# Hybrid attention stepped by head pair, with its output projection split by inner halves

## The reference, cut to what matters

```python
h = x
n = rms_norm(h, attn_norm[0])
proj = n @ w_in                                  # 1024 x 3080
oa = dilated_attention(rope(qa)*s, rope(ka), va) # 8 heads of 64
ob = forgetting_attention(qb*s, kb, vb, logf)    # 8 heads of 64
h = h + concat([oa, ob]) @ w_out                 # 1024 x 1024
h = h + conv_glu_ffn(rms_norm(h, ffn_norm[0]), ...)
...
```

## Time and profile before

| | |
|---|---|
| median of 3 runs | 2890.99 us |
| the profiled execution | 2890.38 us |
| its span, first to last instruction | 2888.4 us |
| TensorE busy | 2715.4 us, 94% |
| VectorE / ScalarE / GpSimd busy | 60% / 36% / 35% |
| mean granted TensorE clock | 0.961 of full |
| hybrid attention | 93.2 to 285 us |
| `out0` gemms | 285 to 328.6 us |
| first feed-forward gemms of layer 0 | from 334 us |

### The profile page before, as it was taken

How to read it: one execution, slowest core, us unless ns; L and a number is a source line. 1 busy time by engine, 2 the same in 40 slices (tenths; PEclk the granted TensorE clock), 3 DMA queues, 4 the chain that set the end, 5 groups by cost and what they waited for, 6 DMA issues and landing times.

```text
span 2888.4 us, 34721 instructions
## 1 busy us (share of the span) xinstructions
PE 2715.4 (94%) x11434; PEld 2001.0 (69%) x11434; DVE 1733.4 (60%) x2250; ACT 1052.6 (36%) x1644; POOL 1018.7 (35%) x383
## 2 busy tenths in 40 slices
PE   8999999999998999999698998999989898899998
PEld 6654788887764678888475465888757644687875
DVE  3645774576486676377558346828635944583672
ACT  3344332233144232232442445323344244432333
POOL 3210344444321244444143123444424411354452
PEclk9997999999998899999899999999999998999999
DMA  4110223232210123232111011222321110122221
GB/s 151 59 45 22 73 95 102 94 106 84 73 55 33 46 93 101 89 101 95 47 52 52 29 44 61 99 89 93 104 66 59 44 44 22 66 94 96 93 98 69
DMA packets 56406, 212.17 MB, mean 73 GB/s; under 512 B 6400, under 2 KB 6656, under 8 KB 56192
## 3 DMA queue, kind: packets, MB, share of 16 engines
q1 hardware_dynamic: 55456, 209.60, 21.8%
q10 hardware_dynamic: 864, 1.44, 0.2%
HBM read 208.92 MB, written 2.10 MB: 73 GB/s over the span
## 4 chain that ended last, share of the span: by engine, by line
PE 74%; DVE 11%; ACT 5%; issue 5%; POOL 4%; DVEq 0%; ACTq 0%; DMA 0%; POOLq 0%; SPq 0%
PE bank_G L501 20%; PE bank_G L503 20%; PE bank_G L502 19%; PE bank_S L1141 5%; POOL wlo L449 3%; PE bank_O L1151 2%; DVE conv_up L764 2%; PE bank_X L1161 2%; PE bank_S L548 1%; ACT whi L474 1%; PE bank_X L1706 1%; DVE mx L2037 1%; DVE prod L784 1%; PE bank_X L833 1%; DVE conv_up L763 1%
## 5 line engine op out<-in xcount | busy, mean ns | idle before, releaser
L449 POOL TENSOR_TENSOR wlo<-raw,whi 128x1024 fp32r<-128x1024 f32 (+1 forms) x361 | 975.9, 2704 | 1739.7 <-ACT whi L474 1739.6
L501 PE MATMUL bank_G<-n_hi,whi 128*128 128x512 f32 x2392 | 975.9, 408 | 63.9 <-DVE n_lo L608 24.7
L503 PE MATMUL bank_G<-n_hi,wlo 128*128 128x512 f32 x2392 | 944.0, 395 | 0.0
L502 PE MATMUL bank_G<-n_lo,whi 128*128 128x512 f32 x2392 | 942.7, 394 | 0.0
L501 PEld LDWEIGHTS bank_G<-n_hi,whi 128*128 128x128 f32 x2392 | 457.3, 191 | 204.3 <-issue 60.0
L474 ACT ACTIVATE whi<-raw 128x1024 fp32r<-128x1024 f32 (+1 forms) x363 | 403.4, 1111 | 349.7 <-PE bank_G L503 349.6
L502 PEld LDWEIGHTS bank_G<-n_lo,whi 128*128 128x128 f32 x2392 | 457.7, 191 | 96.6 <-issue 7.8
L503 PEld LDWEIGHTS bank_G<-n_hi,wlo 128*128 128x128 f32 x2392 | 455.7, 191 | 98.8
L674 DVE SCALAR_TENSOR_TENSOR h<-h,mixed 128x512 f32 (+1 forms) x96 | 70.3, 732 | 397.1 <-ACT mixed L480 397.1
L501 PE MATMUL bank_G<-a_hi,whi 128*128 128x512 f32 x704 | 275.3, 391 | 5.7 <-DVE a_lo L786 3.8
L503 PE MATMUL bank_G<-a_hi,wlo 128*128 128x512 f32 x704 | 274.0, 389 | 0.0
(11 more groups left out here) (271 smaller groups left out, 2659.4 us busy)
## 6 DMA issues: line engine op xcount, KB each, us to landing
raw<-in_w_mix_in SPq DMA_DIRECT2D x42, 512.0 KB, 3.3
raw<-in_w_out SPq DMA_DIRECT2D x32, 512.0 KB, 3.3
raw<-in_w_hyb_in SPq DMA_DIRECT2D x25, 512.0 KB, 3.3
raw<-in_w_diff_in SPq DMA_DIRECT2D x24, 512.0 KB, 3.3
raw<-in_w_up0a SPq DMA_DIRECT2D x22, 512.0 KB, 3.3
raw<-in_w_up0b SPq DMA_DIRECT2D x22, 512.0 KB, 3.3
raw<-in_w_up1a SPq DMA_DIRECT2D x22, 512.0 KB, 3.2
raw<-in_w_up1b SPq DMA_DIRECT2D x22, 512.0 KB, 3.3
```

The lines of the kernel that those rows point to most:

```text
L449: pool.tensor_tensor(b.wlo[:, g.slot, 0:width], b.raw[:, g.slot, 0:width], b.whi[:, g.slot, 0:width], ALU.subtract).then_inc(b.lo_ready, 1)
L501: pe.matmul(out, b.whi[:, g.slot, w], hi[:, k, :], start=(k == 0), stop=False)
L502: pe.matmul(out, b.whi[:, g.slot, w], lo[:, k, :], start=False, stop=False)
L503: mm = pe.matmul(out, b.wlo[:, g.slot, w], hi[:, k, :], start=False, stop=(k == pieces - 1))
```

## The change

1. `out0` becomes two groups of eight half-width tiles: `out0a` (inner channels 0 to 511, the dilated heads) and `out0b` (the forgetting heads). Both add to `h`.
2. The hybrid attention runs 32 units of a head pair (two heads by one query block) in 37 steps, lag 2 in place of 3. The two score matmuls of a step read partitions 0 to 63 and 64 to 127 and write the two slots of `bank_S`. A gemm half (12 matmuls) stands in each of steps 0 to 23; steps 24 to 26 have none; step 27+m has the gemm of `out0a` tile m; steps 35 and 36 have three quarters of `out0b` tiles 0 and 1. `hyb_out_pe` does the rest.
3. No projection's result is copied to `mixed` any more (except in the mixers' inputs): VectorE adds `bank_G` to `h` directly and that evacuates the slot. ScalarE only splits weights there.
4. In `out0b`, ScalarE does the squares, and the next gemm's inputs 0 to 3 are made between the tiles, 4 to 7 after the last.
5. `norm_sum` 1, 2 and 3 move behind the first gemm of the next group.

```diff
-GROUPS = [("hyb_in", B1_IN, W8), ("out0", KD, W8), *ffn_groups(0),
+KH = KD // 2
+GROUPS = [("hyb_in", B1_IN, W8), ("out0a", KD, KH * P), ("out0b", KD, KH * P), *ffn_groups(0),
...
-def first_gemms_n(pe, b, g0, nlo):
+def first_gemms_n(pe, b, g0, nlo, q=None):
     gemm(pe, b, Index(g0), b.n_hi, b.n_lo, KD, lambda k: pe.wait_ge(b.nlo_ready, nlo + k + 1))
+    if q is not None:
+        norm_sum(pe, b, q)
     gemm_n(pe, b, Index(g0 + 1))
...
@@ products_act
-            wait(act, b.resid_done, r0 + k - 1 if k else max(r0 - 1, 0))
-            take(act, b, Index(g0 + k), b.mixed[:, (g0 + k) % 2, :])
+            split_hi(act, b, Index(g0 + k + 2))
...
@@ products_dve
-        dve.wait_ge(b.evacuated, g.at(1))
-        ins = dve.scalar_tensor_tensor(h, h, float(alpha), b.mixed[:, g.slot, :], ALU.mult, ALU.add).then_inc(b.resid_done, 1)
+        dve.wait_ge(b.gemm_done, g.at(1))
+        dve.scalar_tensor_tensor(h, h, float(alpha), b.G[:, g.slot, :], ALU.mult, ALU.add).then_inc(b.evacuated, 1)
...
-LAG = (3, 2, 3, 3)
+LAG = (2, 2, 3, 3)
+EARLY = 6
+PARKED_STEPS = {24: (0, 1), 25: (2, 3), 27: (4,), 29: (5,)}
+OUT_STEP = 27
...
+def hyb_scores_pe(pe, b, a, u):
+    o, i = a.unit(u)
+    if u % NB == 0:
+        qk_ready_pe(pe, b, a, o)
+    wait(pe, b.masked, 2 * u)
+    for x in range(2):
+        q, k = b.qk[a.rows(x), a.tile(o), i * P:(i + 1) * P], b.qk[a.rows(x), a.tile(o) + 4, 0:a.keys(i)]
+        mm = pe.matmul(b.S[:, x, 0:a.keys(i)], q, k, start=True, stop=True)
+    mm.then_inc(b.scored, 1)
...
+    for step in range(a.steps):
+        u, w, t = step, step - a.lag - 1, step - a.lag
+        if u < a.units:
+            hyb_scores_pe(pe, b, a, u)
+        if 0 <= w < a.units and w % NB == NB - 1:
+            hyb_values_pe(pe, b, a, w // NB)
+        if 0 <= t < a.units:
+            hyb_transposes_pe(pe, b, a, t)
...
+        m = step - OUT_STEP
+        if 0 <= m < KD:
+            gemm(pe, b, Index(outa + m), b.n_hi, b.n_lo, KH, (lambda k: pe.wait_ge(b.nlo_ready, 8 + k + 1)) if m == 0 else None)
+        elif KD <= m < KD + 2:
+            hyb_out_part_pe(pe, b, m - KD, range(KH - 1))
...
+def hyb_out_act(act, b):
+    g0, tiles = group_tiles("out0b")
+    for m in range(tiles):
+        split_hi(act, b, Index(g0 + m + 2))
+        act.wait_ge(b.evacuated, g0 + m + 1)
+        if m < KH:
+            gained_hi_act(act, b, "ffn_norm0", m)
+        wait(act, b.resid_summed, m - 1)
+        act.activation(b.sq[:, (m + 1) % 2, :], b.h[:, m, :], ACT.Square).then_inc(b.resid_squared, 1)
+    for m in range(KH, KD):
+        gained_hi_act(act, b, "ffn_norm0", m)
...
+        if 0 <= step - OUT_STEP < KD:
+            residual_dve(dve, b, Index(outa + step - OUT_STEP), step - OUT_STEP)
...
-            norm_sum(pe, b, 1)
-            ffn_pe(pe, b, 0, 16)
-            norm_sum(pe, b, 2)
+            hyb_out_pe(pe, b)
+            ffn_pe(pe, b, 0, 16, 1)
```

More of the change, by code:

```diff
@@ L1045, in plan @@
         self.lead = 2
[L1046 to L1056, removed]
+        self.rotated = 16
+        self.qk0 = FIRST["diff_in"] + 8
+        plan_qk(self)
         order = [("rot", n) for n in range(2 * self.lead - 1)]
@@ new lines, in hyb_values_pe @@
+def hyb_values_pe(pe, b, a, o):
+    for x in range(2):
+        taken_out(pe, b, Index(a.posts[NB * o + NB - 1][x]))
+    wait(pe, b.hyb_taken, min(max(o - 1, 0), EARLY))
+    for j in range(NB):
+        for x in range(2):
+            h = 2 * o + x
+            mm = pe.matmul(b.O[a.rows(x), o % 2, j * P:T], b.v[:, j, h * DH:(h + 1) * DH], b.pt[:, x, j, j * P:T],
+                           start=(j == 0), stop=(j == NB - 1), skip_group_check=True)
+            if j == NB - 1:
+                mm.then_inc(b.headed, 1)
@@ new lines, in hyb_transposes_pe, with hyb_fox_pe @@
+def hyb_transposes_pe(pe, b, a, t):
+    o, i = a.unit(t)
+    for x in range(2):
+        p = Index(a.posts[t][x])
+        pe.wait_ge(b.scaled, 2 * t + x + 1)
+        wait(pe, b.x_free[p.slot], p.turn())
+        for j in range(i + 1):
+            mm = pe.transpose(b.X[:, p.slot, j * P:(j + 1) * P], b.probs[:, a.small(t, x), j * P:(j + 1) * P], b.k["ident"])
+        mm.then_inc(b.posted, 1)
+def hyb_fox_pe(pe, b, a, o):
+    pe.wait_ge(b.fox, 5)
+    for x in range(2):
+        p, n = Index(a.fox_posts[o][x]), 2 * o + x - 8
+        pe.wait_ge(b.x_free[p.slot], p.turn())
+        pe.matmul(b.X[:, p.slot, :], b.k["ident"][0:8, n:n + 1].to_broadcast([8, P]), b.negc[0:8, :],
+                  start=True, stop=True).then_inc(b.posted, 1)
@@ L1282, in hyb_attention_pe @@
 def hyb_attention_pe(pe, b):
-    qk_ready_pe(pe, b, ATT_HYB, 0)
+    a, outa, outb = ATT_HYB, FIRST["out0a"], FIRST["out0b"]
     taken_out(pe, b, Index(POST_HYB + 7))
[L1286 to L1295, removed]
@@ new lines, in hyb_out_part_pe, with hyb_out_pe @@
+def hyb_out_part_pe(pe, b, m, part):
+    gemm(pe, b, Index(FIRST["out0b"] + m), b.n_hi, b.n_lo, KH,
+         (lambda k: pe.wait_ge(b.nlo_ready, 8 + KH + k + 1)) if m == 0 else None, part, KH)
+def hyb_out_pe(pe, b):
+    g0, tiles = group_tiles("out0b")
+    for m in range(2):
+        hyb_out_part_pe(pe, b, m, range(KH - 1, KH))
+    for i, g, g_next in pairs(pe, g0 + 2, tiles - 2):
+        gemm(pe, b, g, b.n_hi, b.n_lo, KH, None, None, KH)
+        gemm(pe, b, g_next, b.n_hi, b.n_lo, KH, None, None, KH)
@@ new lines, in hyb_out_act @@
+def hyb_out_act(act, b):
+    g0, tiles = group_tiles("out0b")
+    for m in range(tiles):
[7 more added lines that the diff above has]
+        gained_hi_act(act, b, "ffn_norm0", m)
+def hyb_attention_dve(dve, b, link):
+    a, outa = ATT_HYB, FIRST["out0a"]
+    for step in range(a.steps):
+        u, t, w = step, step - a.lag + 1, step - a.lag - 3
+        scaling = 0 <= t < a.units
+        if scaling:
+            dve.wait_ge(b.exped, t + 1)
+            n = a.small(t, 0)
+            r = b.rden[:, n:n + 2]
+            link.mark(dve.reciprocal(r, b.den[:, n:n + 2]))
+        for x in range(2):
+            if u < a.units:
+                o, i = a.unit(u)
+                if x == 0:
+                    dve.wait_ge(b.scored, u + 1)
+                    if u >= a.buffers:
+                        dve.wait_ge(b.posted, a.posts[u - a.buffers][1] + 1)
+                    if o >= 4:
+                        dve.wait_ge(b.fox_masked, u - 4 * NB + 1)
+                n, keys = a.small(u, x), a.keys(i)
+                dve.tensor_tensor_reduce(out=b.probs[:, n, 0:keys], in0=b.S[:, x, 0:keys], in1=a.mask(b, o, i, x)[:, 0:keys],
+                                         scale=-1.0, scalar=BIG, op0=ALU.add, op1=ALU.min,
+                                         accum_out=b.nmax[:, n:n + 1]).then_inc(b.masked, 1)
+            if scaling:
+                if x == 0:
+                    link.settle()
+                y = b.probs[:, a.small(t, x), 0:a.keys(a.unit(t)[1])]
+                dve.tensor_scalar(y, y, r[:, x:x + 1], None, ALU.mult).then_inc(b.scaled, 1)
+        if w >= 0 and w % NB == NB - 1 and w // NB >= EARLY:
+            o = w // NB
@@ new lines, in residual_dve, with hyb_out_dve @@
+def residual_dve(dve, b, g, m):
+    dve.wait_ge(b.gemm_done, g.n + 1)
+    h = b.h[:, m, :]
+    dve.tensor_tensor(h, h, b.G[:, g.slot, :], ALU.add).then_inc(b.evacuated, 1)
+def hyb_out_dve(dve, b, link):
+    g0, tiles = group_tiles("out0b")
+    link(dve.memset(b.acc[:, :], 0.0))
+    for m in range(tiles):
+        dve.wait_ge(b.evacuated, FIRST["out0a"] + m + 1)
+        residual_dve(dve, b, Index(g0 + m), m)
+        if 1 <= m <= KH:
+            gained_lo_dve(dve, b, "ffn_norm0", 16, m - 1)
+        if m:
+            dve.wait_ge(b.resid_squared, m)
+            wait(dve, b.resid_summed, m - 1)
+            dve.tensor_tensor(b.acc[:, :], b.acc[:, :], b.sq[:, m % 2, :], ALU.add).then_inc(b.resid_summed, 1)
+    dve.wait_ge(b.resid_summed, tiles - 1)
+    dve.sem_inc(b.acc_ready, 1)
+    dve.wait_ge(b.resid_squared, tiles)
+    dve.sem_inc(b.last_ready, 1)
+    for m in range(KH, KD):
+        gained_lo_dve(dve, b, "ffn_norm0", 16, m)
@@ L2285, in _ @@
             hyb_attention_dve(dve, b, link)
[L2286 removed]
+            hyb_out_dve(dve, b, link)
             rope2_dve(dve, b, link)
@@ L2413, in arrays_of @@
                                         *[(k * D + P * t, P) for t in range(8) for k in range(2)]))
-    v["out0"], v["out1"] = weight_tiles(x["hyb_w_out"][0]), weight_tiles(x["diff_w_out"][0])
+    v["out0a"], v["out0b"] = (weight_tiles(half) for half in np.split(x["hyb_w_out"][0], 2))
+    v["out1"] = weight_tiles(x["diff_w_out"][0])
     small = []
```

249 lines of the change are left out of this document (146 added, 103 removed).

## The result

Five runs after the change gave 2864.9 to 2880.3 us, median **2872.5 us**, beside 2892.6 us for the kernel before in the same comparison: a ratio of 0.9934, 95% interval 0.9913 to 0.9955. So it is faster, by 0.66%, some 20 us where 42 were forecast, and above the range's upper end of 2868. The profiled execution took 2870.7 us.

What follows compares the result with a forecast made beforehand. TensorE, busy 94% of the span, was taken as the bound. Gains of 20.8 (scores abreast), 14.9 (step 24 on) and 6.0 (norms and projections), 41.7 us, off 2890.4 gave 2848.7, stated as 2849; range 2830 to 2868.

Steps and rivals of the forecast that it cites:

- Scores two abreast: Hybrid attention, steps 0 to 23: a pair's scores cost 2.95 us instead of 5.90; stretch 125.2 us, gain 20.8.
- check by another engine: Hybrid pair steps: VectorE, with one GpSimd hold, is busy 9.2 of 10.4 us over two steps, so doesn't stop the gain.
- Rival 1: Hybrid attention: score saving doesn't arrive because VectorE's masks and holds set the step; 2871 us; chance 0.16 shared with another rival.
- Rival 3: Hybrid attention: slower, lag of two steps doesn't cover the hand-over and TensorE waits in each step; 2950 us; chance 0.03.
- second way to 20.9: Hybrid pair period from the differential attention's 19.74 us a head plus 1.1 us for ten transposes: 20.8 us.
- Step 24 to the end of `out0`: Hybrid attention's last steps and `out0`: 74.5 us against 89.4, a gain of 14.9.
- Steps 24 to 26: Hybrid attention steps without gemm: walked by queue as 13 to 16 us in sum, taken as 15 us.
- norm of layer 0: From the end of `out0` to the feed-forward gemm: four `n_lo` made earlier, 21.7 us now, gain about 2.
- second norm: Moving the norm sum behind the first gemm fills TensorE's wait for the last square: gain 1.8 us.
- Third norm: After `out1`: first gemm still waits for the first `n_lo`, the moved sum comes on top; taken as -2 us.
- lower clock that was named as a chance: Third norm, after `out1`: up to 2 us more lost if the clock falls in the longer idle.
- Fourth norm and second block: Direct residual takes 0.55 us off tails at fourth and four layer norms, +2.7; earlier weight splits at `out1` to `out3`, +1.5.

Runs made afterwards that it cites:

- last kernel: Changed kernel with the half gemm ahead of the rotation, copies between the exponentials, and third norm sum back ahead of the first gemm: 2837.3 us, ratio 0.9822.
- two-edit kernel: Changed kernel with the half gemm ahead of the rotation and the `pt` copies between the two exponentials: 2841.9 us, ratio 0.9825.
- rest_only: Kernel before with only the direct residual add and the moved norm sums (parts 3 and 5): 2877.1 us, ratio 0.9956.

## Why the prediction was wrong

Direction right, mechanism of the gain right, size twice too large.

- **The step that failed** is "Scores two abreast", where it sets the pair period at 20.8 to 20.9 us. It priced the rotations and forgetting rows by their own 0.87 us and gave them no wait. The change gives both slots of `bank_X` to the transposes of one step, and in the first step of a pair the copies that free them stand behind the second exponential. The text did see the slot, but only for step 24 ("then two forgetting rows that wait for the slots"), not for the eight earlier steps with a rotation or forgetting rows. TensorE waited in seven of them, 13.7 us in all.
- **The check by another engine was the wrong check.** It counted VectorE's busy time (9.2 of 10.4 us with the hold) and found room. There was room: the same 82 us of VectorE work fit into 126 us in the last kernel. What mattered was where in the chain the hold fell: between the two masks, so that everything that frees a slot came 1.8 us later. Rival 1 (VectorE's masks and holds set the step) had named the hold, but scores waited for a mask once in the stretch, and the score saving did arrive. Rival 3 (every step waits for its hand-over) didn't happen either: the wait was in seven of 24 steps, at TensorE's program order.
- **A coincidence.** Rival 1's price, 17.7 + 6 us on 2848.7, gives 2872.4 (the text says 2871), which is the time measured. Its mechanism isn't what the runs show; the two sizes happen to be alike.
- **The second way to 20.9** took the differential attention as the model of the pair step. That stage transposes its two branches as one tile, into one slot, and leaves the other to the rotation. It has the same scores and masks, and lacks the resource that was scarce.
- **Of the 20 us** between the changed kernel's 147.7 and the two-edit kernel's 127.7, 13.7 us are waits at L827 and L1351. The other 6.3 us are busy time, 131.6 against 125.3 us for the same matmuls: the mean clock was 0.93, where the kernel before had 0.99. Behind the two waits of 4.0 us and the three of 1.2 to 1.3 us matmuls ran at the lower level, behind those of 1.4 and 0.4 us they didn't. The 2.4 us for a mask in step 1, which the forecast doesn't have either, stay in every one of these reorderings.
- **Scores abreast**: 17.7 us forecast, 17.2 measured by taking it away. The Trainium skill, TensorEngine Tiling (Array Packing), section PSUM Bottleneck, warns that evacuating PSUM may become the limit; it did not here. With the order mended, VectorE's masks let TensorE run at 21.0 us a pair.
- **Step 24 to the end of `out0`**: 74.5 forecast, 76.2 measured, 73.7 in the last kernel. Steps 24 to 26 took 16.6 us for 15. The tiles of `out0a` hid inside the attention as told.
- **The norm of layer 0**: 21.7 to 18.2 us, 3.5 gained for 2 forecast.
- **From there to the end of `out1`**, with the second norm: 659.4 us before, 657.8 after, 1.5 gained for 2.3 forecast.
- **Third norm**: 2 us lost by the forecast; from the last matmul of `out1` to the first of `down1a` the profiles have 125.3 us before and 128.9 after, 3.6 lost, and 124.6 with the sum back. The lower clock that was named as a chance came in every profile of a kernel with the sum moved.
- **Fourth norm and second block**, from the first gemm of `down1a` to the end: 1753.5 us before, 1747.0 after, 6.5 gained where the tails and two starts made 3.7.
- Parts 3 and 5 alone are worth 11 us (2887.9 to 2877.1) by medians, where the prediction had 4 to 5. The profile of `rest_only` is of its slowest run (2889.9 us, the other four 2874.6 to 2878.6), so the excess isn't pinned to a stage.

## What to carry to other kernels

When a step is doubled up, count the slots that its doubled output takes and ask who else wants one: the operation that finds none waits in program order, and work that is ready waits behind it. Put ready work ahead of an operation that waits for a slot, and the release of a slot ahead of work that waits for something else; here two reorderings without any new work gave 31 us, more than the 20 us of the change itself. A stage that serves as a model must be compared resource by resource, not only by its instructions.

## What the runs showed of the hardware

A GpSimd tensor operation held a VectorE scale that reads and writes SBUF until it was done (2.09 us for 0.28 us of work), and stopped doing so when GpSimd's operation shrank from 2.35 to 0.24 us; the masks, which read `bank_S`, took 0.69 us beside it (the kernel with the masks first). Two float32 score matmuls of contraction 64 and 512 columns on different halves of the partitions took 1.13 us together, on the same half 1.98 us. After 4.0 us of idle, and after 1.3 us followed by the forgetting rows, TensorE's matmuls ran at the lower level (0.63 us in place of 0.39), so a wait cost more than its length. In the two-edit kernel they did so once behind forgetting rows that had waited for nothing.
